# Last four tiles of a row product taken bank by bank, the two token halves normed and turned apart, some low parts moved to GpSimd

## The reference, cut to what matters

```python
for l in range(DEPTH):                      # 2 layers: retention, then differential attention
    x = layer_norm(DN_ALPHA * x + mix, ln_g[l, 0], ln_b[l, 0])
    x = layer_norm(DN_ALPHA * x + peer_ffn(x, ...), ln_g[l, 1], ln_b[l, 1])
...
x = x + 0.5 * swiglu(rms_norm(x, ffn1_norm), w1, w3, w2)
x = x + (gate_a * y_a + gate_b * y_b) @ w_out          # mixer on rms_norm(x, mix_norm)
x = x + 0.5 * swiglu(rms_norm(x, ffn2_norm), w1, w3, w2)
return rms_norm(x, final_norm)
```

## Time and profile before

| | |
|---|---|
| median of 3 runs | 2798.86 us (2798.58 to 2801.27) |
| profiled execution, span from first to last instruction | 2796.1 us |
| PE busy | 2703.3 us (97%) |
| DVE, ACT, POOL busy | 1871.7, 1254.9, 708.2 us |
| PE waits before transposes (line 436) | 24.6 + 23.4 us at the joints, 7.9 us at the start |
| mean granted TensorE clock | 0.986 |

### The profile page before, as it was taken

One profiled execution on the slowest core, in us unless ns is written; L12 is line 12 of the kernel. 1 busy time (PEld: TensorE's weight loads), 2 busy tenths in 40 slices (PEclk: granted clock), 3 DMA queues, 4 the chain that ended last, 5 costly groups with the idle time before them and its releaser, 6 DMA issues.

```text
span 2796.1 us, 43604 instructions
## 1 busy us (share of the span) xinstructions
PE 2703.3 (97%) x17504; PEld 2453.2 (88%) x17504; DVE 1871.7 (67%) x3258; ACT 1254.9 (45%) x1774; POOL 708.2 (25%) x314
## 2 busy tenths in 40 slices
PE   8998999999999998879999999999989999999998
PEld 7888999999888886679999998888879988888997
DVE  5655898777666666757987776666665567666554
ACT  4343455333455454534463334554544465343443
POOL 0000898666000000005996662000000020000000
PEclk9999999999999999989999999999999999999999
DMA  6554555444666664335554446666645553113554
GB/s 206 166 188 159 169 180 168 141 142 138 203 194 192 194 195 141 111 131 164 180 178 142 140 140 188 192 193 194 194 146 182 189 167 130 53 61 106 164 183 158
DMA packets 124280, 451.61 MB, mean 162 GB/s; under 512 B 13856, under 2 KB 13984, under 8 KB 123952
## 3 DMA queue, kind: packets, MB, share of 16 engines
q1 hardware_dynamic: 122256, 441.57, 49.8%
q0 software_dynamic: 1824, 7.25, 0.8%
HBM read 446.67 MB, written 2.10 MB: 160 GB/s over the span
## 4 chain that ended last, share of the span: by engine, by line
PE 90%; DVE 5%; POOL 3%; ACT 1%; issue 1%; DMA 0%; DVEq 0%; SPq 0%; POOLq 0%; ACTq 0%
PE ps L450 13%; PE ps L451 13%; PE ps L452 13%; PE ps L485 11%; PE ps L486 11%; PE ps L487 11%; PE ps L590 4%; PE ps L472 3%; PE ps L474 3%; PE ps L473 3%; POOL ring_r L2229 2%; PE ps L715 2%; DVE W L1443 2%; DVE x L1443 1%; PE ps L436 1%
## 5 line engine op out<-in xcount | busy, mean ns | idle before, releaser
L1008 ACT ACTIVATE hi<-ring 128x1024 fp32r<-128x1024 f32 x830 | 868.6, 1052 | 403.7 <-PE ps L452 278.2
L2229 POOL TENSOR_TENSOR ring_r<-ring,hi 128x1024 fp32r<-128x1024 f32 x260 | 660.2, 2550 | 1271.9 <-ACT hi L1008 1270.8
L450 PE MATMUL ps<-xT_r,hi 128*128 128x256 f32 x3248 | 935.4, 288 | 4.9 <-DVE ring_r L1466 2.9
L451 PE MATMUL ps<-xT_r,hi 128*128 128x256 f32 x3248 | 920.6, 283 | 0.0
L452 PE MATMUL ps<-xT_r,ring_r 128*128 128x256 f32 x3248 | 920.5, 283 | 0.0
L1466 DVE TENSOR_TENSOR ring_r<-ring,hi 128x1024 fp32r<-128x1024 f32 x570 | 692.0, 1223 | 282.0 <-ACT hi L1008 281.6
L450 PEld LDWEIGHTS ps<-xT_r,hi 128*128 128x128 f32 x3248 | 625.0, 192 | 8.9 <-DVE ring_r L1466 3.3
L451 PEld LDWEIGHTS ps<-xT_r,hi 128*128 128x128 f32 x3248 | 625.4, 193 | 0.7 <-issue 0.7
L452 PEld LDWEIGHTS ps<-xT_r,ring_r 128*128 128x128 f32 x3248 | 624.5, 192 | 0.0
L485 PE MATMUL ps<-hi,oht_r 128*128 128x512 f32 x1040 | 404.9, 389 | 1.4 <-DVE ring_r L1466 1.2
L486 PE MATMUL ps<-ring_r,oht_r 128*128 128x512 f32 x1040 | 404.6, 389 | 0.0
(11 more groups left out here) (227 smaller groups left out, 2702.7 us busy)
## 6 DMA issues: line engine op xcount, KB each, us to landing
ring<-in_peer_u SPq DMA_DIRECT2D x256, 512.0 KB, 3.5
ring<-in_peer_v SPq DMA_DIRECT2D x256, 512.0 KB, 4.2
ring<-in_f SPq DMA_DIRECT2D x132, 512.0 KB, 3.5
ring<-in_ret_vg SPq DMA_DIRECT2D x32, 512.0 KB, 3.5
ring<-in_peer_q SPq DMA_DIRECT2D x32, 512.0 KB, 3.5
ring<-in_ret_qk SPq DMA_DIRECT2D x16, 512.0 KB, 3.5
ring<-in_ret_out SPq DMA_DIRECT2D x16, 512.0 KB, 3.5
ring<-in_in_shift SPq DMA_DIRECT2D x14, 512.0 KB, 3.5
```

What stands on the lines that cost most here:

```text
L450: pe.matmul(o, h, xT[:, k, 0:256], start=k == 0, stop=False)
L451: pe.matmul(o, h, xT[:, k, 256:512], start=False, stop=False)
L1008: hid.done(a.activation(hi[m % NH][:, :], ring[j % NR][:, :], ACT.Copy), j)
L2229: lo_p.done(p.tensor_tensor(low_part[j % NR][:, :], ring[j % NR][:, :], as32(hi[m % NH][:, :]), ALU.subtract), j)
```

## The change

It does five things. (a) `mat_out` takes the last four tiles bank by bank, with one exchange (bank 1 of the first of them comes before bank 0 of the last). (b) `layer_norm`, `rms` and the final norm treat the first 128 tokens while the second 128 are still multiplied. (c) Before `peer` and `diff` x is turned by token half (`halves`): ACT copies the first half's transposes twice, once rounded into `xT`, once plain into a buffer `XF`, and POOL subtracts (`first_half`); DVE does the second half (`second_half`). (d) The second tile of a new stage (after joints 1 to 6) has its low part made by POOL instead of DVE. (e) The gains and offsets of the layer norms are loaded into areas of their own (`GB`), at other times.

```diff
@@ weight_tiles
-            add("peer_q", l * 16 + i, "V" if i else "P")
+            add("peer_q", l * 16 + i, "V" if i > 1 else "P")
...
@@ tensor_program
+            def halves(stage, src, ready):
+                for tt in range(2):
+                    for c in (0, 4):
+                        b = bank(stage, "T", tt, c)
+                        pe.wait_ge(*ready(tt * 2 + c // 4))
+                        for j in range(4):
+                            ins = pe.transpose(b[:, j * 128:j * 128 + 128], src(tt, c + j), ident)
+                        mm.done(ins, stage, "T", tt, c)
...
-                last = len(tiles) - (0 if fine else 2)
+                end = len(tiles) - 1
+                last = end + 1 - (0 if fine else 4)
...
-                    for q in range(4):
-                        for k in (last, last + 1):
-                            if q == 0:
-                                awaited(k)
-                            ins = quarter(k, q)
-                            if q == 3 and k == last:
-                                mm.done(ins, "eaten", tiles[k])
-                        mm.done(ins, name, "out", q)
-                    mm.also("eaten", tiles[-1])
+                    turns = [(q, last + k) for q in range(4) for k in range(4)]
+                    turns[3], turns[4] = turns[4], turns[3]
+                    for q, k in turns:
+                        if q == 0:
+                            awaited(k)
+                        ins = quarter(k, q)
+                        if k == end:
+                            mm.done(ins, name, "out", q)
+                        elif q == 3:
+                            mm.done(ins, "eaten", tiles[k])
+                    mm.also("eaten", tiles[end])
@@ scalar_program
+            def half_parts(stage, tt, copy=None):
+                for c in (0, 4):
+                    pv = c4(ps(stage, "T", tt, c))
+                    a.wait_ge(*at(mm, stage, "T", tt, c))
+                    act.done(a.activation(xT[:, c:c + 4, tt * 128:tt * 128 + 128], pv, ACT.Copy), stage, "Th", tt, c)
+                    if copy is not None:
+                        act.done(a.activation(c4(copy[:, c * 128:c * 128 + 512]), pv, ACT.Copy), stage, "Tc", c)
+                        empties(act, stage, "T", tt, c)
@@ vector_program, layer_norm
+                added(0)
+                added(1)
+                spread(0)
+                v.wait_ge(*loaded(("gb", l, i)))
+                centred(0)
+                normed(0)
+                added(2)
+                added(3)
+                spread(1)
+                centred(1)
+                if between is not None:
+                    between()
+                normed(1)
@@ vector_program, rms
-                for k in range(3):
-                    added(k)
+                added(0)
+                added(1)
                 mean_square(stage, 0)
+                added(2)
+                scaled(stage, xs, 0)
                 added(3)
-                scaled(stage, xs, 0)
                 mean_square(stage, 1)
                 scaled(stage, xs, 1)
@@ gpsimd_program
+            def after_norm(l, i, tile, stage):
+                root(0, "ln", l, i)
+                split(tile)
+                root(1, "ln", l, i)
+                first_half(stage, XF[i])
+                split(tile + 1)
+
+            def after_rms(stage, tile):
+                root(0, "rms", stage)
+                split(tile)
+                root(1, "rms", stage)
+                split(tile + 1)
...
+            after_norm(0, 1, TILE["diff_q", 0], "diff")
             load("diff", [(D_lamt, prow(9, 256))], [at(dve, "norm", 0, 1)])
```

More of the change, by code:

```diff
@@ L437, in parts, with by_pair, by_half, mat_t @@
                     mm.done(ins, stage, "T", c)
[L439 removed]
+            def halves(stage, src, ready):
[6 more added lines that the diff above has]
+                        mm.done(ins, stage, "T", tt, c)
+            def by_pair(stage):
+                return lambda k: [at(dve, stage, "Tl", k)] if k % 2 == 0 else []
+            def by_half(stage):
+                return lambda k: [at(pool, stage, "Tl", k), at(dve, stage, "Tl", k)] if k % 4 == 0 else []
+            def mat_t(tiles, stage, *name, among=tuple(range(8)), first=None, behind=None):
                 b = bank(*name, among=among)
@@ L446, in mat_t @@
                     for k in range(8):
-                        if first and j == 0 and k % 2 == 0:
-                            pe.wait_ge(*at(dve, stage, "Tl", k))
+                        if first is not None and j == 0:
+                            for w in first(k):
+                                pe.wait_ge(*w)
                         h, l = hi[n][:, k * 128:k * 128 + 128], low_part[i % NR][:, k * 128:k * 128 + 128]
@@ L457, in mat_t, with mat_n @@
                         behind(j)
-            def mat_n(tiles, stage, *name, among=tuple(range(8)), first=False):
+            def mat_n(tiles, stage, *name, among=tuple(range(8)), first=None):
                 bs = [bank(*name, tt, among=among) for tt in range(2)]
@@ L463, in mat_n @@
                     pe.wait_ge(*low(i))
-                    if first:
-                        pe.wait_ge(*at(dve, stage, "Tl", 2 * q))
+                    if first is not None:
+                        for w in first(2 * q):
+                            pe.wait_ge(*w)
                     for k in range(2):
@@ L535, in retention @@
                     for z in range(2):
-                        mat_t([TILE["ret_qk", (h * 2 + z) * 2 + j] for j in range(2)], "x0", "ret_qk", h, z, first=h + z == 0)
+                        mat_t([TILE["ret_qk", (h * 2 + z) * 2 + j] for j in range(2)], "x0", "ret_qk", h, z, first=None if h + z else by_pair("x0"))
                         if z and h:
@@ L566, in peer @@
             def peer(l):
-                parts(("peer", l), lambda tt, c: tok3(x, tt, c), 8, ready=lambda c: at(dve, "norm", l, 0, 3 if c else 2))
+                halves(("peer", l), lambda tt, c: tok3(x, tt, c), lambda k: at(dve, "norm", l, 0, k))
                 for i in range(0, 16, 2):
-                    mat_t([TILE["peer_q", l * 16 + i + j] for j in range(2)], ("peer", l), "peer_q", l, i, first=i == 0)
+                    mat_t([TILE["peer_q", l * 16 + i + j] for j in range(2)], ("peer", l), "peer_q", l, i,
+                          first=None if i else by_half(("peer", l)))
                 B7 = tuple(range(7))
@@ L608, in diff @@
                 HI4, LO4 = (4, 5, 6, 7), (0, 1, 2, 3)
-                parts("diff", lambda tt, c: tok3(x, tt, c), 8, ready=lambda c: at(dve, "norm", 0, 1, 3 if c else 2))
+                halves("diff", lambda tt, c: tok3(x, tt, c), lambda k: at(dve, "norm", 0, 1, k))
                 def group(z, nb):
                     yield from mat_n([TILE[D_names[z], nb * 4 + j] for j in range(4)], "diff", "diff_p", z, nb,
-                                     first=z + nb == 0, among=HI4)
+                                     first=None if z + nb else by_half("diff"), among=HI4)
                 def turned(z, nb):
@@ L718, in shift @@
                 def shift(i):
-                    mat_t([TILE["in_shift", 2 * SHIFT[i] + j] for j in range(2)], "mix", "shift", i, among=RW, first=i == 0)
+                    mat_t([TILE["in_shift", 2 * SHIFT[i] + j] for j in range(2)], "mix", "shift", i, among=RW,
+                          first=None if i else by_pair("mix"))
                 def head_sums(name, src):
@@ L1727, in diff @@
             def diff():
-                parts("diff", 8, xT)
+                second_half("diff")
                 v.wait_ge(*loaded("diff"))
@@ L2246, in peer, with first_half, root @@
                     split(TILE["peer_u", l * 128 + i] + 2)
-                gains(l, 1, mm, "peer_u", l, 126)
-                split(TILE["peer_v", l * 128 + 127] + 1)
-                roots("ln", l, 1)
+                gains(l, 1, dve, "prep", l, 71)
+            def first_half(stage, copy):
+                for c in (0, 4):
+                    p.wait_ge(*at(act, stage, "Tc", c))
+                    pool.done(p.tensor_tensor(xT[:, c:c + 4, 256:384], c4(copy[:, c * 128:c * 128 + 512]), as32(xT[:, c:c + 4, 0:128]),
+                                              ALU.subtract), stage, "Tl", c)
+            def root(tt, *name):
+                power(rs_r[:, tt:tt + 1], *name, tt)
+            def after_norm(l, i, tile, stage):
[9 more added lines that the diff above has]
+                split(tile + 1)
             n = CONW["ident"]
```

99 lines of the change are left out of this document (53 added, 46 removed).

## The result

The changed kernel takes 2810.19 us in the median of 5 runs (2808.03 to 2810.46), the kernel before on the same chip 2799.21 us; the ratio is 1.0036 (95% interval 1.0026 to 1.0047). That is slower by more than the 0.2% that can be told, and 1.7 us above the range.

What follows compares the result with a forecast made beforehand. TensorE, busy 97% of the span, was taken as the bound, with the winnable waits at the joints. Terms -2.3 -0.3 -2.3 -2.0 +5.5 +5.1 -0.9 +2.0 = +4.8 us on 2796.1 gave a 2803.5 us median, range 2794.5 to 2808.5.

Steps and rivals of the forecast that it cites:

- joints 1 to 6: Places where TensorE waits ahead of transposes after a row product; 48 us in seven waits, including one short turn inside a stage.
- I take DVE first: Joint 4, after the last root: VectorE's first scaling piece precedes GpSimd's subtraction; 0.5 us left, joint gains 2.0 us.
- POOL first: Rival: GpSimd takes its turn before VectorE's scaling at joints 4, 5, 6; 1.7, 1.1, 1.1 us more, 2807.5; 1.5 in 10.
- E: End of the row product at a joint: start of its last matmul plus the 0.23 us pitch.
- I take **+2: TensorE's clock: slower matmuls after more broken work and longer idle stretches at joints 5 and 6 cost 2 us.
- the upper bound of +5: TensorE's clock: most it could cost, joint 1's loss of about 1.0 us repeated at five more joints.
- Layer norms: Joints 1 to 4: halves shorten the chain before multiplying; joints 1 and 3 gain 2.3 us each, joint 4 2.0.
- Multiplying begins in effect at E+9.3: Joints 1 and 3: multiplying starts then instead of at E+11.6, gaining 2.3 us each.
- Joints 5 and 6: Squares wait behind ScalarE's later high part, and VectorE's scalings behind GpSimd: losses of 5.5 and 5.1 us.
- the turn at the first scaling: Joint 5: the first half's scaling waits for GpSimd's first-tile low part (until E+4.1), ending at E+5.0.
- Joint 2: Starts 2.6 us earlier, but the later lambdas transfer costs 2.2 at the third tile, `peer_v` 0.16; gains 0.3 us.
- Joint 7: No next tile; the last square starts the last mean at once, not behind the first scaling; gains 0.9 us.

Runs made afterwards that it cites:

- e2: The changed kernel with the second tile's low part back on VectorE at joints 4, 5 and 6: 2803.59 us, ratio 1.0012.
- e5: The changed kernel plus unused float32 matmuls on TensorE ahead of the transposes at joints 1 to 3 (six, then one): 2811.3 us, 1.0043.
- e1: The changed kernel with ScalarE making the next stage's first high part only after the third of four squares at joints 5 and 6: 2801.87 us, 1.0004.
- e7: The changed kernel with the first half's low parts on VectorE at joints 1 to 3, GpSimd's second-tile low part after the norm: 2809.34 us, 1.0034.
- e11: The kernel before with the last four tiles bank by bank and ScalarE's squares ahead of the high part at joints 5 and 6: 2802.79 us, 1.001.
- e16: e9 with the first half's low parts on GpSimd again, behind VectorE's norm, and all second tiles' low parts on VectorE: 2789.3 us, 0.9961.
- e9: e8 plus unused float32 matmuls on TensorE: five between the halves' transposes at joints 1 to 3, ten at joint 4, four at 5 and 6: 2789.49 us, 0.9958.
- e8: The changed kernel with e1, e2 and e7 together, and the lambdas' transfer issued ahead of the second low part: 2792.12 us, 0.9977.
- e13 to e15: The kernel before with five, nine and seventeen VectorE aggregations instead of one at joint 2, delaying it 1.0, 1.9, 3.8 us: 2802.01, 2800.68, 2807.65 us.

## Why the prediction was wrong

**The direction and the main mechanism held, and two steps failed.** The forecast had +4.8 us on the span, and it was +12.3. Of the 7.5 us between them, 3.9 are GpSimd's turn at the three scalings of joints 4, 5 and 6 (1.6, 1.2 and 1.1), 2.9 are TensorE's clock (1.3 at joints 1 to 3 and 3.6 in the two stretches inside `diff` and the mixer, against the +2 of the forecast), and 0.8 lie elsewhere; joint 7 gives 0.1 back.

- *First failed step, the order at the scalings*: "I take DVE first" at joint 4, and the same order at the second halves of joints 5 and 6. GpSimd was first at all three, by 0.01 to 0.05 us, and VectorE's two pieces took 3.1 us instead of 1.0. By e2 the turn cost 2.1 us at each. The rival "POOL first" is what came true. Its argument "POOL needs no signal for its own next instruction" was the right one. Against it stood that GpSimd would have to wait for the high part (E+7.6) at joints 5 and 6; at joint 5 ScalarE had made it at E+7.1, just ahead of the root's end at E+7.2.
- *Second failed step, the clock*: "I take **+2**, since only joints 5 and 6 get a longer idle stretch". While the granted clock was 0.50, TensorE was busy for 43 us in the kernel before and for 55 us in the changed one; half of the difference, 6 us, is what the clock cost more. Joints 5 and 6, whose idle stretch did get longer, have next to none of it (0.3 us); joints 1 to 3, whose idle stretches got shorter, have 2.9, and the two stretches in `diff` and the mixer, far from any joint, 3.4. Joint 4 gave 0.9 back. That is above the upper bound of +5, five more losses like joint 1's, which left out stretches far from the joints. That the clock behind an idle stretch costs what it does is shown at joints 1 to 3 (e5); why the shorter stretches cost more is not.
- *Layer norms.* The chain was right: "Transposes at E+6.5 and E+8.2" were at 6.3 and 8.0, the last low part of x was ready at E+10.4 (10.7), and the 1.2 us for a 128x512 subtraction was 1.25 (two in 2.50 us in e5). "Multiplying begins in effect at E+9.3" holds for the full clock: in e5 the second tile comes at E+12.2, one tile of 2.9 us behind E+9.3. In the changed kernel the whole first tile ran at 0.50, and joints 1 and 3 gained 1.5 us and not 2.3.
- *Joints 5 and 6*: the reading that ScalarE's order makes the squares late was right, and so was the turn at the first scaling (e1: 4.1 us each for both).
- *Joint 2*: -0.6 for -0.3. VectorE waits for the lambdas:

```profile
1069.18 0.29 DVE L1482 TENSOR_TENSOR W<-W 128x128 f32<-128x128 f32 x1 [3.07 <-DMA W<-in_prow]
```

  TensorE waited only 0.35 us behind it, where 2.2 were forecast: its first two tiles ran partly at the lower clock, so it came to the third that much later. In e5, where they were faster, it waited 4.07 us.
- *Joint 7*: -1.0 for -0.9.

The Trainium skill's rule cited ahead (SBUF — State Buffer, "Who interferes with whom") agrees with the traces: VectorE's norm takes 4.65 us beside GpSimd's subtractions and 2.96 without (e7), and its two scalings 3.08 us behind one and 1.01 without (e2).

What stays open: what makes the slow stretches in `diff` and the mixer come and go, and why the clock cost more at joints 1 to 3. Part (e) of the change had no experiment of its own; the trace of the changed kernel shows no wait for those loads.

## What to carry to other kernels

- When work is brought forward on one engine, read every queue that stands behind the moved signal: here a tile eaten 6 us later delayed the high part that takes its place, and that held up squares on ScalarE and, in e11, a root on GpSimd. There one repair without the other gave nothing.
- A subtraction moved to GpSimd was not free where it began just ahead of a VectorE pass over SBUF: at joints 4 to 6 it cost 2.1 us each (e2). Started behind the norm (e16) it left VectorE's three passes at 2.96 us, and brought the first product from E+8.7 (e9) to E+7.8.
- A change of some us in a kernel that is 97% TensorE must be checked for matmuls that became longer. A delay of 3.8 us cost 7.5 (ratio 1.0018 to 1.0039, where the delay alone is 1.0014); for 1.0 and 1.9 us nothing clear of noise was measured.

## What the runs showed that I had not expected

- Matmuls for nobody during the idle stretches kept the granted clock at 1.00 over joint 1's first tile (e5), where it was 0.50 for 5.3 us, but gave only 2.6 us (5 by the ratios) on e8 and nothing that can be told on the kernel before.
- The same code in `diff` and in the mixer was multiplied at 1.00 in one trace and at 0.50 in another (the kernel before and e13 to e15, the changed kernel and e5), though the edit between them was hundreds of us away or, for `diff`, only a delay.
- Removing a turn can be worth nothing: e7 took 1.7 us off VectorE's norm at each of three joints, gave it 1.7 us of low parts instead, and won 0.9 us in all.
